# Rope rows of four tiles turned together beside the first projection, and three ada blocks on VectorE

## The chip, the core and the metric

One core of one Trainium2 chip runs the whole kernel. The metric is the device time of one execution in microseconds (us): before the change 2828.47, the median of three (2826.29 to 2839.01).

## What is computed

Two transformer blocks follow each other on 256 tokens of width 2048; the change is in the first. It needs a modulation vector, a projection, and rope on a part of its rows:

```python
mod = jax.nn.silu(c) @ w_ada[l] + b_ada[l]              # 2048 x 12288, 24 blocks of 512 columns
shift_a, scale_a, gate_a, shift_f, scale_f, gate_f = jnp.split(mod, 6, axis=-1)
h = rms_norm(x, g_attn_pre[l]) * (1.0 + scale_a[:, None]) + shift_a[:, None]
proj = h @ w_in[l]                                      # 2048 x 5456
d_q, d_k, d_v, s_q, s_k, s_v, i_q, i_k, i_w = parts     # cut from proj
rot = d // ROPE_FRACTION                                # 16 of 64 or 32 of 128 dims of a head
rotated = jnp.concatenate([x1 * cos - x2 * sin, x2 * cos + x1 * sin], axis=-1)
```

d_q, d_k, i_q and i_k have heads of 64 dims, of which rope turns 16; s_q and s_k have heads of 128, of which it turns 32. The indexer then scores keys with i_q, i_k and i_w, each query keeps 64 keys, and two kinds of attention follow.

## The kernel before

Activations lie transposed: proj is 43 tiles of 128 rows (dims) by 256 tokens, `T_DQ` 0, `T_DK` 8, `T_DV` 16, `T_SQ` 24, `T_SK` 32, `T_SV` 33, `T_IQ` 34, `T_IK` 42. All large products use float32 split in two: ScalarE rounds a weight unit into w_hi (`split`, L753), VectorE takes w_lo = raw - w_hi (`rest`, L1153), and TensorE runs three matmuls for each tile (`dense`, L1692 to L1694): x_hi w_hi, x_lo w_hi, x_hi w_lo. A unit is 4 x 128 rows by 512 columns of weights, 1 MB (1.05 million bytes).

SyncE loads the units into `raw`, a ring of four buffers (`RAW` = 4, `load`, L524): load k waits for `raw_free` of load k - 4, and all loads go through the one queue in order. w_hi and w_lo are rings of two.

The first projection walks the contraction in four parts (`K16`) and each part over 11 units of columns in the order `ORDER_IN1`; the first is a tail of 336 columns, then come the units of s_k, s_v, i_q, of s_q, of d_q, d_k and d_v. Part 0 writes proj (ScalarE, L898), parts 1 to 3 add to it (VectorE, L1311). Between them go blocks of w_ada: 512 columns are four loads (quarters), and TensorE multiplies each quarter by silu(c) right after a unit (`ada_quarter`, L1727, for units 0 to 7 of a part), ScalarE copies the sum row (`take_row`, L826), TensorE turns it into columns (`ada_columns`, L1739) and ScalarE stores them (`take_columns`, L831). So two blocks pass in each part. In the stream of loads w_in and w_ada alternate:

```python
for n, j in enumerate(ORDER_IN1):
    load(*unit("w_in", K16[part], j * COLS, in1_width(n)))
    if n < 8:
        ada(n % 4, ADA_ORDER[ADA_IN1 + 2 * part + n // 4] * COLS)
```

Parts 1 to 3 need the next quarter of x, modulated and split, which VectorE makes behind units 8 and 9 of the part before (`modulate_quarter`, `apply`).

The program of VectorE for one unit u is: `rest(u + 1)`, then the four additions of unit u, each behind its `tile_done`. The program of ScalarE is: `split(u + 1)`, then the copies that are due. TensorE runs `dense(u)`, then the ada quarter.

When all 44 units are done, rope follows for 18 steps (`turns1`): VectorE multiplies two tiles by the sines (`rotate_sin`, L1338), TensorE multiplies the product by a rotation matrix (`rotate`, L1853), GpSimd multiplies the tiles by the cosines (`rotate_cos`, L677), and VectorE adds (L1330). Rows that rope leaves alone pass through with cosine 1 and sine 0. Two ada blocks are run by TensorE between these steps. Then TensorE turns the values (`turn_values`, L1875, copied by VectorE, L1353), the indexer scores 16 heads (L1890, L1891 on TensorE; relu, L914, on ScalarE; the weighted sum, L1367, on VectorE) with two more ada blocks beside it, and the attention heads follow, with three.

After the heads, blocks of w_ada are summed by VectorE in another place (`ada_unit`, L1179 and L1181, four fused multiply-adds a quarter).

Of the kernel before, what the change touches and what calls it, by code (L numbers as in the profile page):

```python
# [36 lines left out]
COLS = 512  # L37
UK = 4
RAW = 4
# [18 lines left out]
C_ID, C_R64, C_R128, C_R64D, C_I64D, C_RM, C_COL, C_J = 0, 128, 256, 384, 512, 640, 704, 768  # L58
C_F64, C_F128, C_FM, C_ONE = 896, 897, 898, 899
# [25 lines left out]
def constants():  # L85
# [11 lines left out]
    c[:, C_R64:C_R64 + P] = rotation(64, 8, 2)  # L97
    c[:, C_R128:C_R128 + P] = rotation(128, 16, 1)
    c[:64, C_R64D:C_R64D + P] = np.tile(rotation(64, 8, 1), (1, 2))
    c[:64, C_I64D:C_I64D + P] = np.tile(np.eye(64), (1, 2))  # L100
# [13 lines left out]
    c[:, C_F64] = np.where(p % 64 < 16, freq(500000.0, 16)[p % 8], 0)  # L114
    c[:, C_F128] = np.where(p < 32, freq(500000.0, 32)[p % 16], 0)
# [24 lines left out]
ADA_ORDER = [0, 4, 1, 5, 2, 6, 3, 7, *range(8, 24)]  # L140
ADA_IN1, ADA_HEADS, ADA_OUT1, ADA_MLP1 = 2, 10, 17, 20
UNIT_HEADS = 4 * 19
UNIT_OUT1 = UNIT_HEADS + 4 * (ADA_OUT1 - ADA_HEADS)


def in1_unit(part, n):

    return 19 * part + (2 * n if n < 8 else 8 + n)
# [62 lines left out]
def program(nc, a):  # L211
    with ExitStack() as ctx:
# [12 lines left out]
        def over(start, *parts):  # L225
# [43 lines left out]
        gpad = place("gpad", [P, 4, NC])  # L269
        diag = place("diag", [P, 2, 4, P], at=gpad_at)  # L270
# [10 lines left out]
            arena, ("proj", [P, 43, S]), ("rope1", [P, 4, S]), ("posf", [P, S]), ("causal", [P, 3 * P]),  # L281
# [3 lines left out]
        vtok_at, sheets_at = arena + 4 * (43 * S + 4 * S + S + 3 * P), end - 12288  # L285
        assert vtok_at + 8 * D <= end - 12288 - 4 * 8 * S
        (rope_s, rope_c), _ = over(sheets_at, ("rope_s", [P, 2, 2, S]), ("rope_c", [P, 2, 2, S]))
# [48 lines left out]
        gain_ready = sem("gain_ready")  # L336
        lam_summed, lam_exp = sem("lam_summed"), sem("lam_exp")
# [124 lines left out]
        def pair(k):  # L462
            return rope1[:, k, :].unsqueeze(1).broadcast_to([P, 2, S])

        R64, R128 = cst[:, C_R64:C_R64 + P], cst[:, C_R128:C_R128 + P]
        RM = cst[0:64, C_RM:C_RM + 64]
        turns1 = [(proj[:, t:t + 2, :], pair(1), pair(0), R64, None, proj[:, t:t + 2, :])
                  for t in (*range(T_DQ, T_DV, 2), *range(T_IQ, T_IK, 2))]
        turns1 += [(proj[:, t:t + 2, :], pair(3), pair(2), R128, None, proj[:, t:t + 2, :])
                   for t in range(T_SQ, T_SK, 2)]  # L470
        turns1 += [(proj[:, T_SK, :], rope1[:, 3, :], rope1[:, 2, :], R128, None, proj[:, T_SK, :]),
                   (proj[0:64, T_IK, :], rope1[0:64, 1, :], rope1[0:64, 0, :], cst[0:64, C_R64D:C_R64D + P],
                    cst[0:64, C_I64D:C_I64D + P], ikk[:, :])]
# [40 lines left out]
        def _(sp):  # L514
# [92 lines left out]
        def _(pool):  # L607
# [60 lines left out]
            angles(posf[:, :], (C_F64, C_F128), P, S, rope1, sq[:, 0, 0:S], sq[:, 1, 0:S])  # L668
# [17 lines left out]
            def projected1():  # L686
                pool.wait_ge(bank_freed, BLOCKS_IN1 * 4 + 4)
                pool.wait_ge(rope_ready, 4)
            rotate_cos("one", projected1)
# [49 lines left out]
        def _(act):  # L739
# [143 lines left out]
            split(UK * in1_width(0))  # L883
            for u in range(44):
                part, n = divmod(u, 11)
                if n in (5, 9):
                    take_columns(ADA_IN1 + 2 * part + (n == 9))
# [5 lines left out]
                if n in (4, 8):  # L893
                    take_row(ADA_IN1 + 2 * part + (n == 8))
# [11 lines left out]
            for s in (ADA_HEADS, ADA_HEADS + 1):  # L906
                take_row(s)
                take_columns(s)

            for h in range(16):  # L910
# [234 lines left out]
        def _(dve):  # L1145
# [150 lines left out]

            ur.at = in1_unit(0, 0)
            rest(UK * in1_width(0))
            for u in range(44):
# [43 lines left out]
            dve.wait_ge(bank_freed, BLOCKS_IN1 * 4 + 4)  # L1343
            dve.wait_ge(rope_ready, 4)
            rotate_sin("one")

# [797 lines left out]
```

## Time and profile before

| | |
|---|---|
| median of 3 runs | 2828.47 us |
| the profiled execution, its own time | 2830.93 us |
| its span in the profile | 2829.1 us |
| TensorE busy | 2626.5 us, 93% |
| VectorE, ScalarE, GpSimd busy | 49%, 37%, 10% |
| mean granted clock of TensorE | 0.952 |
| loads of w_ada, w_in | 88 of 1 MB from the ring, 68 of 1 MB and 8 smaller ones (both projections) |

The span runs from the first instruction to the last. Times below are us from its start. PE is TensorE, PEld its weight loads, DVE VectorE, ACT ScalarE, POOL GpSimd, SPq and ACTq the instructions by which SyncE and ScalarE issue transfers. PEclk is the granted clock of TensorE as a share of 2.4 GHz. In the timeline a line gives start, length, engine, source line and operation, and in brackets the idle time before it and who ended it.

### The profile page before, as it was taken

The numbers are of one execution on the slowest core, as the hardware profiler recorded it, in microseconds if no ns is written. First come the engines' busy times: TensorE is split into PE (matmuls) and PEld (weight loads), VectorE is DVE, ScalarE is ACT, GpSimd is POOL, SyncE is SP. The second block draws the span as 40 slices with busy tenths as digits, with TensorE's granted clock in tenths as the row PEclk, the third lists the DMA queues.
The fourth block names the chain that finished last, engine by engine and source line by source line (L and its number), as shares of the span: only waits on it lengthen the run. The fifth ranks groups of instructions, "written<-read, shape, count | busy, mean of one in ns | idle before, by whom it ended". The sixth has DMA issues, their size and how long they took to land. (4 is left out here: it accounts for less than half of the span.)

```text
span 2829.1 us, 48216 instructions
## 1 busy us (share of the span) xinstructions
PE 2626.5 (93%) x20124; PEld 2402.9 (85%) x20124; DVE 1399.1 (49%) x1817; ACT 1043.2 (37%) x1327; POOL 296.6 (10%) x372
## 2 busy tenths in 40 slices
PE   5999989969999999999879979798899999999998
PEld 3888836959999999999869947358899999999998
DVE  2455565946674444344353354524455555554443
ACT  3533224334334343333233325323244444443332
POOL 4000043230000000012122000101200000000000
PEclk8999999989999999999989979778999999999999
DMA  7777765836785555555535411003455555554553
GB/s 280 263 248 274 272 238 196 316 108 215 244 289 193 179 183 188 167 191 178 174 87 178 148 38 60 30 1 117 136 175 178 182 180 181 187 178 160 182 185 111
DMA packets 260590, 501.56 MB, mean 177 GB/s; under 512 B 16160, under 2 KB 23035, under 8 KB 260219
## 3 DMA queue, kind: packets, MB, share of 16 engines
q1 hardware_dynamic: 249888, 492.99, 52.0%
q10 hardware_dynamic: 10603, 7.18, 0.9%
q8 instruction: 70, 1.15, 0.2%
q14 instruction: 29, 0.24, 0.0%
HBM read 498.05 MB, written 2.10 MB: 177 GB/s over the span
## 5 line engine op out<-in xcount | busy, mean ns | idle before, releaser
L1153 DVE TENSOR_TENSOR w_lo<-raw,w_hi 128x2048 fp32r<-128x2048 f32 (+2 forms) x386 | 862.6, 2235 | 1077.1 <-ACT w_hi L753 1077.1
L1692 PE MATMUL bank<-x_hi,w_hi 128*128 128x256 f32 (+3 forms) x4608 | 1313.8, 285 | 51.8 <-DVE w_lo L1153 17.8
L1693 PE MATMUL bank<-x_lo,w_hi 128*128 128x256 f32 (+3 forms) x4608 | 1308.7, 284 | 0.0
L1694 PE MATMUL bank<-x_hi,w_lo 128*128 128x256 f32 (+3 forms) x4608 | 1308.4, 284 | 0.0
L753 ACT ACTIVATE w_hi<-raw 128x2048 fp32r<-128x2048 f32 (+2 forms) x386 | 719.1, 1864 | 1075.5 <-PE bank L1694 945.1
L1692 PEld LDWEIGHTS bank<-x_hi,w_hi 128*128 128x128 f32 (+1 forms) x4608 | 875.5, 190 | 87.9 <-issue 37.7
L1694 PEld LDWEIGHTS bank<-x_hi,w_lo 128*128 128x128 f32 (+1 forms) x4608 | 876.5, 190 | 0.0
L1693 PEld LDWEIGHTS bank<-x_lo,w_hi 128*128 128x128 f32 (+1 forms) x4608 | 872.9, 189 | 0.0
L1692 PE MATMUL bank<-hid_hi,w_hi 128*128 128x256 f32 x1408 | 400.0, 284 | 7.9 <-POOL hid_lo L648 6.6
L1693 PE MATMUL bank<-hid_lo,w_hi 128*128 128x256 f32 x1408 | 399.1, 283 | 0.0
L1694 PE MATMUL bank<-hid_hi,w_lo 128*128 128x256 f32 x1408 | 399.0, 283 | 0.0
L1692 PEld LDWEIGHTS bank<-hid_hi,w_hi 128*128 128x128 f32 x1408 | 270.9, 192 | 9.5 <-issue 7.9
L1693 PEld LDWEIGHTS bank<-hid_lo,w_hi 128*128 128x128 f32 x1408 | 271.0, 192 | 0.0
L1694 PEld LDWEIGHTS bank<-hid_hi,w_lo 128*128 128x128 f32 x1408 | 270.9, 192 | 0.0
L648 POOL TENSOR_TENSOR hid_lo<-gpad,hid_hi 128x256 f32 x88 | 60.4, 720 | 1000.8 <-ACT hid_hi L1003 501.0
L677 POOL TENSOR_TENSOR rope_c<-proj,rope 128x512 f32<-128x512 f32 (+3 forms) x27 | 36.3, 1358 | 635.3 <-DVE proj L1311 303.1
L1181 DVE SCALAR_TENSOR_TENSOR ada_acc<-raw,csilu,ada_acc 128x512 f32<-128x512 f32 x105 | 84.2, 802 | 3.0
L1807 PE MATMUL bank<-rstd_rows,cst 16*128 16x272 f32 (+5 forms) x92 | 40.7, 621 | 31.8 <-DVE rstd_rows L1252 31.8
L1727 PE MATMUL bank<-raw,csilu 128*32 128x512 f32 x480 | 65.6, 619 | 1.3 <-ACT mod L831 1.3
L1807 PEld LDWEIGHTS bank<-rstd_rows,cst 16*128 16x128 f32 (+3 forms) x92 | 27.0, 303 | 43.2 <-DVE rstd_rows L1252 34.9
L876 ACT ACTIVATE x_hi<-tmp 128x258 fp32r<-128x258 f32 (+2 forms) x62 | 25.9, 423 | 92.2 <-DVE tmp L1282 92.2
L1311 DVE TENSOR_TENSOR proj<-proj,bank 128x256 f32<-128x256 f32 (+1 forms) x129 | 47.5, 415 | 19.0 <-PE bank L1694 19.0
(261 smaller groups left out, 1553.2 us busy)
## 6 DMA issues: line engine op xcount, KB each, us to landing
raw<-in_w_ada SPq DMA_DIRECT2D x88, 1024.0 KB, 5.2
raw<-in_w_gate SPq DMA_DIRECT2D x88, 1024.0 KB, 5.2
raw<-in_w_up SPq DMA_DIRECT2D x88, 1024.0 KB, 5.2
raw<-in_w_in SPq DMA_DIRECT2D x68, 1024.0 KB, 5.7
raw<-in_w_down SPq DMA_DIRECT2D x64, 1024.0 KB, 5.0
raw<-in_w_down SPq DMA_DIRECT2D x32, 768.0 KB, 4.4
raw<-in_w_o SPq DMA_DIRECT2D x16, 1024.0 KB, 6.0
raw<-in_w_out SPq DMA_DIRECT2D x16, 1024.0 KB, 5.1
```

The costliest lines, as they stand in the source:

```text
L648: pool.tensor_tensor(lo, gpad[:, m, 0:S], hi, ALU.subtract).then_inc(hid_low, 1)
L677: pool.tensor_tensor(rope_at(rope_buf(which, 1, src), r, src), src, cos, ALU.mult).then_inc(r_cos, 1)
L753: act.activation(w_hi[ps][:, 0:width], raw[slot][:, 0:width], ACT.Copy).then_inc(hi_ready, 1)
L876: act.activation(hi, tmp[:, (n["first"]["split"] + k) % 2, 0:n["n"]], ACT.Identity, bias=shift if shift is not None else 0.0).then_inc(n_h ...
L1153: dve.tensor_tensor(w_lo[ps][:, 0:width], raw[slot][:, 0:width], w_hi[ps][:, 0:width], ALU.subtract).then_inc(raw_free[slot], 1)
L1181: ins = dve.scalar_tensor_tensor(ada_acc[:, :], w, s, ada_acc[:, :], ALU.mult, ALU.add)
L1311: dve.tensor_tensor(t_, t_, bank[m][0:rows, 0:S], ALU.add).then_inc(bank_freed, 2 if tail and m == 2 else 1)
L1692: pe.matmul(out, wh[:, k, c], hi(k0 + k), start=a0, stop=False)
L1693: pe.matmul(out, wh[:, k, c], lo(k0 + k), start=False, stop=False)
L1694: ins = pe.matmul(out, wl_[:, k, c], hi(k0 + k), start=False, stop=z)
L1727: ins = pe.matmul(bank[7][32 * k:32 * k + 32, :], csilu[:, 4 * q + k:4 * q + k + 1].broadcast_to([P, 32]), w[:, k * COLS:(k + 1) * COLS], ...
L1807: ins = pe.matmul(spread_row(name, g, P, cols), ident[0:groups, g:g + 1].broadcast_to([groups, P]), rstd_rows[0:groups, 0:cols], start=Tru ...
```

## The change

It has two parts.

Rope. Only the rows that turn are moved. ScalarE issues small transfers inside the fourth part of the projection that gather the 16 (or 32) rows of each head into full tiles: `rows_iq`, `rows_sq`, `rows_d` hold 128 rows by two tiles of 256 tokens, `rows_x` the 16 rows of i_k and the 32 of s_k. There are five such sets (`turns1` has 5 steps in place of 18). For each, GpSimd now makes both products, TensorE one rotation, VectorE one addition (`add_rows`), and ScalarE issues transfers that scatter the rows back, for i_k into the doubled key tile `ikk`. There are 30 gathers and 33 scatters, of 16 or 32 rows each. Four sets are turned beside units 5 to 10 of the fourth part, the fifth (d_k) behind the turning of the values, and the last two scatters are issued ahead of the indexer's first relu.

Ada. Parts 0 to 2 take three blocks each in place of two; the third is summed by VectorE (`ada_beside`) behind the additions of units 1, 3, 5 and 7, a quarter each, and TensorE makes its columns behind unit 10. Part 3 keeps two. The rope stage has none left in place of two, the index stage one in place of two, the heads three as before.

```diff
-ADA_ORDER = [0, 4, 1, 5, 2, 6, 3, 7, *range(8, 24)]
-ADA_IN1, ADA_HEADS, ADA_OUT1, ADA_MLP1 = 2, 10, 17, 20
+ADA_ORDER = [0, 4, 1, 5, 8, 2, 6, 9, 3, 7, *range(10, 24)]
+ADA_IN1, ADA_LAST, ADA_INDEX, ADA_HEADS, ADA_OUT1, ADA_MLP1 = 2, 11, 13, 14, 17, 20
+def beside(part):
+    return part < 3
+def ada_of(part, which):
+    return ADA_IN1 + 3 * part + which
...
                     if n < 8:
-                        ada(n % 4, ADA_ORDER[ADA_IN1 + 2 * part + n // 4] * COLS)
-            for s in range(ADA_HEADS, ADA_OUT1):
+                        ada(n % 4, ADA_ORDER[ada_of(part, n // 4)] * COLS)
+                        if beside(part) and n % 2:
+                            ada(n // 2, ADA_ORDER[ada_of(part, 2)] * COLS)
+            for s in range(ADA_INDEX, ADA_OUT1):
...
-            rotate_cos("one", projected1)
+            for r, (src, sin, cos, _, _, _) in enumerate(turns1):
+                pool.wait_ge(rows_in[r], 16 * (2, 8, 4, 8, 8)[r])
+                if r >= 2:
+                    pool.wait_ge(r_sum, r - 1)
+                    pool.wait_ge(r_out, r - 1)
+                pool.tensor_tensor(rope_at(rope_s, r, src), src, sin, ALU.mult).then_inc(r_sin, 1)
+                pool.tensor_tensor(rope_at(rope_c, r, src), src, cos, ALU.mult).then_inc(r_cos, 1)
...
+            def gather(r, rows, tiles, dst):
+                for j in range(4):
+                    for g in range(32 // rows):
+                        act.dma_start(dst[32 * j + rows * g:32 * j + rows * g + rows, :, :],
+                                      proj[64 * g:64 * g + rows, tiles + j:tiles + 8:4, :]).then_inc(rows_in[r], 16)
...
+            def rope_rows(n):
+                done = {3: 2, 4: 3, 6: 5, 8: 7, 10: 9}
+                if n in done:
+                    act.wait_ge(bank_freed, 4 + 4 * (33 + done[n]))
...
+                elif n == 4:
+                    gather(1, 16, T_IQ, rows_iq)
+                elif n == 6:
+                    gather(2, 32, T_SQ, rows_sq)
...
+                elif n == 8:
+                    gather(3, 16, T_DQ, rows_d[:, 0:2, :])
+                elif n == 9:
+                    scatter(1, 16, T_IQ, rows_iq)
+                elif n == 10:
+                    scatter(2, 32, T_SQ, rows_sq)
+                    gather(4, 16, T_DK, rows_d[:, 2:4, :])
...
+                if n == 0 and part:
+                    take_columns(ada_of(part - 1, 2))
...
+            scatter(3, 16, T_DQ, rows_d[:, 0:2, :])
+            scatter(4, 16, T_DK, rows_d[:, 2:4, :])
...
+            def ada_beside(s, q):
+                at_ = ada_unit_at(s, q)
...
+                dve.wait_ge(raw_loaded[at_ % RAW], 16 * (at_ // RAW + 1))
+                for k in range(4):
...
+                        ins = dve.scalar_tensor_tensor(acc_beside[:, :], w, c_, acc_beside[:, :], ALU.mult, ALU.add)
...
+                ins.then_inc(raw_free[at_ % RAW], 1)
+            def add_rows(r):
+                src = turns1[r][0]
+                dve.wait_ge(r_sum, r + 1)
+                dve.wait_ge(r_cos, r + 1)
+                dve.tensor_tensor(src, turned_at(r, src), rope_at(rope_c, r, src), ALU.add).then_inc(r_out, 1)
...
+                if beside(part) and n in (1, 3, 5, 7):
+                    ada_beside(ada_of(part, 2), n // 2)
...
+                if part == 3 and n in (6, 7, 9):
+                    add_rows({6: 0, 7: 1, 9: 2}[n])
+            add_rows(3)
...
-            rotate_sin("one")
...
             take_values(0, 9, 2, lambda j: vtok[:, :, j, :])
+            add_rows(4)
...
+                if n == 10 and beside(part):
...
+                    for j in range(4):
+                        ins = pe.matmul(bank[7][:, j:j + 1], acc_beside[:, P * j:P * j + P], one(), start=True,
+                                        stop=True)
+                    ins.then_inc(ada_cols, 1)
+                if part == 3 and n in (5, 6, 8, 10):
+                    rotate_rows({5: 0, 6: 1, 8: 2, 10: 3}[n])
...
-            rotate("one")
...
+            rotate_rows(4)
+            pe.wait_ge(r_out, 4)
...
+            pe.wait_ge(rows_back[0], 16 * 5)
+            pe.wait_ge(rows_back[1], 16 * 8)
```

`rotate_rows(r)` is one matmul of the whole set by a rotation matrix. GpSimd also zeroes `rows_x` and copies the sine and cosine rows for it (four copies of 32 rows) once, early.

## Rows read from the trace of the kernel before

**Rows 1.** Stretches: length, busy times by engine, PEclk, DMA share, GB/s.
```profile
60.00:353.30 293.30, 285.79 (x2339) 254.96 (x2337) 151.15 (x205) 104.90 (x117) 0.00 (x0) 0.99 0.77 266
353.30:391.40 38.10, 34.02 (x146) 11.84 (x150) 29.78 (x46) 1.54 (x5) 28.45 (x18) 0.96 0.62 221
...
366.00:371.00 5.00, 4.40 (x16) 1.95 (x14) 4.29 (x6) 0.45 (x2) 4.60 (x4) 1.00 1.03 377
```
**Rows 2.** Waits, 60 to 353: us in total, times, longest.
```profile
ACT w_hi L753 <- DMA raw<-in_w_in: 94.3, 23, 8.0
```
**Rows 3.** Waits of the load queue, 60 to 353.
```profile
SPq L524 <- PE bank L1727: 187.3, 31, 8.5
```
**Rows 4.** Timeline of two units in part 2, from 211 to 232.
```profile
211.77 0.39 PE L1692 MATMUL bank<-x_hi,w_hi 128*128 128x256 f32 x1
...
218.65 0.39 PE L1692 MATMUL bank<-x_hi,w_hi 128*128 128x256 f32 x1
218.78 0.37 SPq L524 DMA_DIRECT2D raw<-in_w_ada  x1
219.19 0.51 SPq L524 DMA_DIRECT2D raw<-in_w_in  x1
...
226.57 1.92 ACT L753 ACTIVATE w_hi<-raw 128x2048 fp32r<-128x2048 f32 x1 [4.20 <-DMA raw<-in_w_in]
228.52 2.29 DVE L1153 TENSOR_TENSOR w_lo<-raw,w_hi 128x2048 fp32r<-128x2048 f32 x1 [2.50 <-ACT w_hi L753]
230.73 1.41 DVE L1311 TENSOR_TENSOR proj<-proj,bank 128x256 f32<-128x256 f32 x4
```
**Rows 5.** Transfers, 100 to 360: count, KB each, median us to landing.
```profile
raw<-in_w_in SPq DMA_DIRECT2D x32, 1024.0 KB, 7.4
raw<-in_w_ada SPq DMA_DIRECT2D x29, 1024.0 KB, 5.1
```
**Rows 6.** Timeline of VectorE in the output projection: one ada quarter.
```profile
513.32 3.11 DVE L1181 SCALAR_TENSOR_TENSOR ada_acc<-raw,csilu,ada_acc 128x512 f32<-128x512 f32 x4
```
**Rows 7.** Timeline of TensorE at the start of part 1.
```profile
136.57 0.36 PE L1692 MATMUL bank<-x_hi,w_hi 128*128 128x256 f32 x1 [3.74 <-DVE proj L1311]
```
**Rows 8.** The stretch behind that gap, columns as in the first group.
```profile
137.00:142.00 5.00, 5.00 (x32) 5.00 (x31) 3.04 (x4) 0.00 (x0) 0.00 (x0) 0.66 0.68 240
```
**Rows 9.** Timeline of TensorE: columns of one ada block.
```profile
340.43 0.95 PE L1739 MATMUL bank<-cst,ada_acc 128*128 128x1 f32 x8
```
**Rows 10.** Timeline from the last addition through the rope stage.
```profile
352.88 0.42 DVE L1311 TENSOR_TENSOR proj<-proj,bank 128x256 f32<-128x256 f32 x1 [0.99 <-PE bank L1694]
...
361.44 1.12 PE L1853 MATMUL bank<-rope_s,cst 128*128 128x512 f32 x2
...
362.60 0.69 DVE L1330 TENSOR_TENSOR proj<-bank,rope_c 128x512 f32<-128x512 f32 x1 [0.76 <-PE bank L1853]
...
365.43 1.65 POOL L677 TENSOR_TENSOR rope_c<-proj,rope 128x512 f32<-128x512 f32 x1 [0.41 <-DVE proj L1330]
```
**Rows 11.** Timeline of ScalarE's queue, 20 to 50: one issue.
```profile
36.39 0.44 ACTq L793 DMA_DIRECT2D packs<-in_ffn_norm_g  x1
```
**Rows 12.** The page, transfers issued by ScalarE: count, KB, us to landing.
```profile
tmp<-in_positions ACTq DMA_DIRECT2D x1, 68.0 KB, 2.8
lam_in<-in_lambda_k ACTq DMA_DIRECT2D x2, 32.0 KB, 9.5
```
**Rows 13.** Timeline of ScalarE in the index stage.
```profile
391.40 0.49 ACT L914 ACTIVATE relu<-bank 128x384 f32<-128x384 f32 x1 [7.16 <-PE bank L1891]
...
400.14 0.49 ACT L914 ACTIVATE relu<-bank 128x384 f32<-128x384 f32 x1 [0.49 <-DVE score L1367]
...
400.99 0.49 ACT L914 ACTIVATE relu<-bank 128x384 f32<-128x384 f32 x1 [0.36 <-DVE score L1367]
...
403.55 0.49 ACT L914 ACTIVATE relu<-bank 128x384 f32<-128x384 f32 x1 [1.22 <-PE bank L1891]
...
405.39 0.49 ACT L914 ACTIVATE relu<-bank 128x384 f32<-128x384 f32 x1 [1.35 <-PE bank L1891]
```

More of the change, by code:

```diff
@@ L96, in rotation @@
         return r.T
[L97 to L100, printed above, removed]
+    c[:, C_RA:C_RA + P] = rotation(16, 8, 8)
+    c[:, C_RB:C_RB + P] = rotation(32, 16, 4)
+    c[0:16, C_RX:C_RX + 16] = rotation(16, 8, 1)
+    c[32:64, C_RX + 32:C_RX + 64] = rotation(32, 16, 1)
     c[:64, C_RM:C_RM + 64] = rotation(64, 32, 1)
@@ L269, in program @@
         gpad = place("gpad", [P, 4, NC])
+        acc_beside = place("acc_beside", [P, COLS], at=gpad_at)
         diag = place("diag", [P, 2, 4, P], at=gpad_at)
@@ L284, in program @@
         assert end <= arena_end, end - arena_end
-        vtok_at, sheets_at = arena + 4 * (43 * S + 4 * S + S + 3 * P), end - 12288
+        vtok_at, sheets_at = arena + 4 * (43 * S + 6 * S + S + 3 * P), end - 12288
         assert vtok_at + 8 * D <= end - 12288 - 4 * 8 * S
+        rows_iq = place("rows_iq", [P, 2, S], at=sheets_at - 32 * S)
+        rows_sq = place("rows_sq", [P, 2, S], at=sheets_at - 24 * S)
+        rows_d = place("rows_d", [P, 4, S], at=sheets_at - 16 * S)
+        rows_x = place("rows_x", [64, S], at=vtok_at + 4 * 2 * 9 * P)
         (rope_s, rope_c), _ = over(sheets_at, ("rope_s", [P, 2, 2, S]), ("rope_c", [P, 2, 2, S]))
@@ L336, in program @@
         gain_ready = sem("gain_ready")
+        rows_in = [sem(f"rope_rows_in{r}") for r in range(5)]
+        rows_back = [sem(f"rope_rows_back{r}") for r in range(5)]
         lam_summed, lam_exp = sem("lam_summed"), sem("lam_exp")
@@ L463, in pair @@
             return rope1[:, k, :].unsqueeze(1).broadcast_to([P, 2, S])
[L465 to L473, printed above, removed]
+        RA, RB, RM = cst[:, C_RA:C_RA + P], cst[:, C_RB:C_RB + P], cst[0:64, C_RM:C_RM + 64]
+        turns1 = [(rows_x[:, :], rope1[0:64, 5, :], rope1[0:64, 4, :], cst[0:64, C_RX:C_RX + 64], None, rows_x[:, :])]
+        turns1 += [(x, pair(k + 1), pair(k), rot, None, x) for x, k, rot in (
+            (rows_iq[:, :, :], 0, RA), (rows_sq[:, :, :], 2, RB), (rows_d[:, 0:2, :], 0, RA), (rows_d[:, 2:4, :], 0, RA))]
         turns2k = [(kpg, rope2[:, 1, :], rope2[:, 0, :], RM, None, kpg)]
@@ L667, in _ @@
             chain(pool.tensor_copy(posf[:, :], pos_i[:, :]))
-            angles(posf[:, :], (C_F64, C_F128), P, S, rope1, sq[:, 0, 0:S], sq[:, 1, 0:S])
+            angles(posf[:, :], (C_FA, C_FB), P, S, rope1[:, 0:4, :], sq[:, 0, 0:S], sq[:, 1, 0:S])
+            pool.wait_ge(rope_ready, 4)
+            pool.memset(rows_x[:, :], 0.0).then_inc(cleared, 1)
+            pool.wait_ge(cleared, 4)
+            for k in range(2):
+                chain(pool.tensor_copy(rope1[0:32, 4 + k, :], rope1[0:32, k, :]))
+                chain(pool.tensor_copy(rope1[32:64, 4 + k, :], rope1[32:64, 2 + k, :]))
             def rotate_cos(which, after):
@@ L893, in _ @@
                 if n in (4, 8):
-                    take_row(ADA_IN1 + 2 * part + (n == 8))
+                    take_row(ada_of(part, int(n == 8)))
+                if part == 3:
+                    rope_rows(n)
                 if part == 0:
@@ L1821, in quarters, with rotate_rows @@
                 return ready
+            def rotate_rows(r):
+                src, _, _, rot, _, dst = turns1[r]
+                pe.wait_ge(r_sin, r + 1)
+                if r >= 2:
+                    pe.wait_ge(r_out, r - 1)
+                flat = rope_at(rope_s, r, src)
+                flat = flat.rearrange("p t n -> p (t n)") if len(flat.shape) == 3 else flat
+                pe.matmul(bank[4 + r % 2][0:dst.shape[0], 0:int(np.prod(dst.shape[1:]))], rot, flat, start=True,
+                          stop=True).then_inc(r_sum, 1)
             ada_quarter(1, 0)
@@ L1834, in _ @@
                 if n in (4, 8):
-                    ada_columns(ADA_IN1 + 2 * part + (n == 8))
+                    ada_columns(ada_of(part, int(n == 8)))
                 if n < 8:
-                    ada_quarter(ADA_IN1 + 2 * part + n // 4, n % 4)
+                    ada_quarter(ada_of(part, n // 4), n % 4)
+                if n == 10 and beside(part):
+                    s = ada_of(part, 2)
+                    last = ada_unit_at(s, 3)
+                    pe.wait_ge(raw_free[last % RAW], last // RAW + 1)
+                    pe.wait_ge(ada_copied, s)
+                    for j in range(4):
+                        ins = pe.matmul(bank[7][:, j:j + 1], acc_beside[:, P * j:P * j + P], one(), start=True,
[3 more added lines that the diff above has]
+                    rotate_rows({5: 0, 6: 1, 8: 2, 10: 3}[n])
                 if u == 10:
@@ L1859, in rotate @@
                     ins.then_inc(r_sum, 1)
-                    if which == "one" and j % 8 in (1, 2, 3, 4) and j < 16:
-                        ada_quarter(ADA_HEADS + j // 8, j % 8 - 1)
-                    elif which == "one" and j % 8 == 7:
-                        ada_columns(ADA_HEADS + j // 8)
-            rotate("one")
             def turn_values(first, tiles, meta):
@@ L1984, in _ @@
             pe.wait_ge(iw_ready, 1)
+            pe.wait_ge(rows_back[2], 16 * 4)
+            for r in (3, 4):
+                pe.wait_ge(rows_back[r], 16 * 8)
             heads(0, 16)
```

97 lines of the change are left out of this document (60 added, 37 removed).

## The prediction

> **What bounds the kernel now.** I read the busy times first: TensorE is busy 93% of the span (table above), so what counts is what makes it wait. Then the stretches that the change touches [rows 1]: the first projection (60 to 353) has TensorE busy for 285.8 of 293.3 us, and the DMA engines at 0.77. The 38.1 us behind it, rope and the turning of the values, are a hole: the loop between VectorE, GpSimd and TensorE. That hole is what the change goes after. A stretch of TensorE at 97% leaves nothing to gain, only to lose, so the next question is what almost makes it wait. The waits say it: ScalarE's w_hi stood 23 times, 94.3 us in all, for a w_in load [rows 2]; and the load queue (SyncE) stood 31 times, 187.3 us, for a TensorE ada quarter [rows 3], that is for a free raw buffer and not for bandwidth. The timeline of one unit [rows 4] gives the slack. Units start every 6.88 us (211.77, 218.65). The w_in load issued at 219.19 is taken up by ScalarE at 226.57; w_hi takes 1.92, w_lo 2.29 and ends at 230.81; the unit that needs it starts two periods after 218.65, at 232.4. So a load is on time by 1.6 us.
>
> **The ring of four raw buffers.** Load k waits until load k-4 has been read, and no load overtakes another. Call W(n), A(n), B the loads of w_in unit n, of TensorE's ada quarter n and of VectorE's. Before, W(n) at place 2n waits for W(n-2) and stands behind A(n-1), which waits for A(n-3): it goes out two units before its use. After, the order is W0 A0 W1 A1 B0 W2 A2 W3 A3 B1 W4. W2 now waits for A0, W3 for A1, W4 for A2: every W(n), n from 2 to 8, waits for A(n-2), so it goes out a whole unit later, with 1.6 us of slack.
>
> Prices. A load alone lands 5.1 us after its issue, the second of a pair 7.4 [rows 5]. In a stretch where the engines were full they moved 377 GB/s [rows 1], 2.8 us for 1.05 MB; so each load ahead in the queue costs 2.8. One ada quarter on VectorE takes 3.1 [rows 6]; I take this, and not the busy 0.8 x 4, because its row holds the chain.
>
> First late unit: A0 is read when the next unit starts (211.77 in part 2). W2 goes out at 211.9, lands 217.0, then 0.1 + 1.92 + 0.03 + 2.29 gives 221.35 against 218.65: **+2.7**, in each of three parts.
>
> Then a cycle over two units, from the end of w_lo(n), n even, in parts 1 and 2. VectorE has the four additions of the unit before, 1.41 [rows 4], queued behind the late w_lo, then B, 3.1: 4.5. Only that frees the slot for A(n+1), and the next B goes out right behind it. W(n+2) is allowed at 7.0, when A(n) has been read, but finds both ahead of it: A lands at 4.65 + 5.1 = 9.75, B at 12.55, W at 15.35. With w_hi and w_lo (4.34) the cycle is 19.7 us, where two units take 13.75: **+5.95**. In part 0 ScalarE does the additions, so 18.3 and **+4.55**. There are three cycles in a part (to n = 4, 6, 8); odd units follow on time; W9 and W10 wait for loads long read. Sum: 3 x 2.7 + 3 x 4.55 + 6 x 5.95 = **+57.5**. Part 3 has no B and runs as now. VectorE's 38 us of ada work itself costs nothing: it lies in waits for w_hi (2.50 us before 228.52 [rows 4], more where w_hi is late).
>
> Smaller terms. In parts 1 and 2 the next unit needs a bank whose addition now stands behind the late w_lo: 2 x 0.4 = **+0.8**. TensorE idles 5 us before each of these units. The one like gap of the trace, 3.74 us before 136.57 [rows 7], was followed by a stretch with the granted clock at 0.66 of full [rows 8], part of it at 1.2 GHz: (1 - 0.66) x 5 = 1.7 us lost. Inside the cycle that is hidden (TensorE has 5 us to spare and W(n+2) is held by the queue), behind the last late unit of a part it is not: 3 x 1.7 = **+5.1**. Columns of the VectorE blocks: eight small matmuls, 0.95 [rows 9], and their gap, three times: **+3.1**. ScalarE's copies for them lie in its idle time; if they did not, 0.2 each. Rotations inside part 3: one of 64 rows and half the columns 0.7 and two of 128x512 at 1.12 [rows 10] and a gap each: **+3.1**. GpSimd's ten products (1.65 each) and VectorE's additions (0.69 each) have 17 us between gather and use and cost nothing there; the last set is below. The 63 issues of ScalarE in and behind part 3 are 0.44 each [rows 11], at most eight or so (3.8 us) in a unit of 6.9 with 1.9 of w_hi: hidden, until the last unit. Their new waits (for an addition two units back, for a sum of rows) stand ahead of the next w_hi, and each is met about a unit before ScalarE comes to it; if one were late, w_hi and with it the next unit would be, us for us beyond 1.6.
>
> Behind the projection. In the coordinates of before: the last addition starts at 352.88 [rows 10], so that of unit 9 ends at 347.6, and the third set of rows is added at 348.3. ScalarE then issues 4 + 8 transfers of 0.47, until 353.95. The last gather lands after 2.8 (68 KB) by the nearest row, 9.5 by the worst (32 KB under full load) [rows 12]; the ring is full and the DMA engines idle there, so I take 2.8: 356.75. GpSimd: sine and cosine, 3.3; the addition 0.7: 360.8. ScalarE issues 8 scatters: 364.6, and the first relu comes at 364.7, where now it is 391.40: **-26.7**. The value turns and TensorE's last rotation end by 360.1, inside that. Index stage: a head beside an ada quarter takes 1.84 (403.55 to 405.39), one without 0.85 (400.14 to 400.99) [rows 13]. Four heads lose their quarter, 4 x 0.99, and TensorE does most of the other four while ScalarE still issues: **-6.8**.
>
> **Sum.** 57.5 + 0.8 + 5.1 + 3.1 + 3.1 - 26.7 - 6.8 = +36.1 on the profiled execution's 2830.9 us: 2867. The median of the runs shown lies 2.5 below that execution: 2864.
>
> What pages say beside this. The Trainium skill, page "TensorE: Matmul & The Clock Gate", section on clock-gate oscillation, holds that a loop which waits for a transfer before each burst of matmuls starts every burst at the slow clock. One row (136.57) agrees, and the gap of 2.7 us before n = 2 would tell if shorter ones do too; this is my third rival. The Trainium skill, page "DMA: Bandwidth & Descriptors", rules for kernel authors, says that transfers under 64 KB are mostly overhead. The 32 KB gathers are such; in the trace 68 KB landed in 2.8 us and 1 MB in 5.1, which agrees, and it speaks against the change.
>
> **Rivals.**
> 1. The ring does not bind: the three loads fit in, as 0.77 of the DMA engines' time seems to leave room. Then -33.5 + 3.1 + 3.1 = -27.3, 2801 us. It decides for faster once the twelve late units cost less than 1.1 us each (27.3 less the 14 of a measurable gain, over 12). Against it: the 1.6 us of slack, and that the place in the queue moves by a full 6.9. Chance 0.09.
> 2. The slot binds, the queue does not (VectorE takes B early, or loads side by side all land in 5.1): 12 late units at 2.7 = 32.4, no cold clock: 32.4 + 0.8 + 6.2 - 33.5 = +5.9, 2834. For it: the B quarter is short; against it: 7.4 for the second of a pair. Chance 0.13.
> 3. The clock falls at each gap and stays low for a whole pair: a unit takes 11.3, A(n) is read at 13.4, the cycle is 23: 9 x 3.3 = +30 and some 8 us more in units 9 and 10, about 2900. Against it: 0.66 over five us is a clock that was low for two thirds of them, not for a pair. Chance 0.10.
> 4. The rows come late (gathers at 9.5, scatters held up): +7 to +15, 2871 to 2879. Chance 0.05.
> My forecast keeps 0.63.
>
> **How the numbers follow.** 2864 is the likeliest case. Its own range, with the landing at 4.0 to 5.5 and no or double clock loss, is 2848 to 2882. The range to hold 8 in 10 reaches down to rival 2 and up to just short of rival 3: 2833 to 2894. A measurement of this kernel tells 0.5% (14 us, 2814 to 2843) from no change: faster is rival 1, 0.09; same is rival 2, 0.13; slower is the rest, 0.78.
>
> **What the profile after would show.** Right: the first quarter of the projection takes some 93 us and the next two 97 each, in place of 74, the fourth some 77; TensorE waits for w_lo before n = 2, 4, 6 and 8, 2.7 and then 5 to 6 us; loads before even units land some 8 us after their issue; the first relu comes about 27 us sooner behind the last addition. Wrong: w_in waits of ScalarE that stay at 94 us in all, or parts of 75 us. If the units wait by 2.7 only, rival 2 holds; if the clock stands near 0.5 through the parts, rival 3.

## The result, and the profile after

The changed kernel takes 2866.01 us (median of 4 runs, 2861.14 to 2872.52) where the kernel before takes 2829.14 (4 runs, 2826.29 to 2839.01): a ratio of 1.0126, interval 1.0091 to 1.016. It is 37 us slower; the forecast was 2864. Its profiled execution took 2862.18 us, with a span of 2860.4 and a mean granted clock of 0.947.

Four marks cut the span: the start of the last addition of the projection, the first relu of the index stage, the causal addition that ends that stage, and the end.

| us from the start | before | after | difference | forecast |
|---|---|---|---|---|
| last addition | 352.9 | 421.4 | +68.5 | +69.6 |
| first relu | 391.4 | 435.3 | +43.9 | +42.9 |
| causal addition | 412.9 | 449.2 | +36.3 | +36.1 |
| end of the span | 2829.1 | 2860.4 | +31.3 | +36.1 |

The stretches of after that answer to [rows 1] (length, busy time and count of PE, PEld, DVE, ACT and POOL, PEclk, DMA share, GB/s):

```profile
60.00:421.40 361.40, 310.95 (x2374) 277.24 (x2375) 187.29 (x255) 105.09 (x120) 12.97 (x13) 0.93 0.74 255
421.40:435.30 13.90, 11.62 (x68) 5.05 (x67) 5.25 (x13) 0.03 (x1) 2.48 (x2) 1.00 0.42 110
435.30:449.20 13.90, 11.42 (x73) 7.32 (x73) 11.74 (x32) 9.29 (x19) 0.00 (x0) 0.88 0.76 248
```

The hole behind the projection shrank from 38.1 to 13.9 us, but the projection has 50 us in which TensorE does nothing (361.4 less 311.0; 7.5 before), a clock of 0.93, and moves fewer bytes per us (255 GB/s, 266 before). More loads, and less bandwidth used: that speaks against the bandwidth as the limit. The waits of after up to 420 us say what it is (total, times, longest), beside [rows 2, 3]:

```profile
SPq L541 <- PE bank L1831: 191.6, 32, 9.7
SPq L541 <- DVE acc_beside L1386: 69.8, 12, 9.8
SPq L541 <- DVE w_lo L1226: 58.2, 13, 8.8
...
ACT w_hi L781 <- DMA raw<-in_w_in: 170.6, 28, 12.4
...
PE bank L1796 <- DVE proj L1412: 34.0, 11, 6.4
PE bank L1796 <- DVE w_lo L1226: 12.5, 5, 4.4
```

ScalarE waits 170.6 us for w_in where it waited 94.3. The load queue has a new wait, twelve times, for VectorE's last product of a quarter (acc_beside): the slot that forecast and code make the path. TensorE's waits for "proj" end with the first addition behind a late w_lo, about 0.5 us after it (w_lo ends at 279.56 below, TensorE goes on at 280.04); so they are waits for w_lo.

Two cycles of part 2 from the timeline of after:

```profile
257.09 2.29 DVE L1226 TENSOR_TENSOR w_lo<-raw,w_hi 128x2048 fp32r<-128x2048 f32 x1 [7.03 <-ACT w_hi L781]
259.30 1.40 DVE L1412 TENSOR_TENSOR proj<-proj,bank 128x256 f32<-128x256 f32 x4
260.62 0.48 DVE L1384 TENSOR_SCALAR acc_beside<-raw,csilu 128x512 f32<-128x512 f32 x1
261.14 2.33 DVE L1386 SCALAR_TENSOR_TENSOR acc_beside<-raw,csilu,acc_beside 128x512 f32<-128x512 f32 x3
...
263.49 0.92 SPq L541 DMA_DIRECT2D raw<-in_w_ada  x2
...
266.80 0.37 SPq L541 DMA_DIRECT2D raw<-in_w_in  x1
...
275.33 1.91 ACT L781 ACTIVATE w_hi<-raw 128x2048 fp32r<-128x2048 f32 x1 [11.39 <-DMA raw<-in_w_in]
...
277.27 2.29 DVE L1226 TENSOR_TENSOR w_lo<-raw,w_hi 128x2048 fp32r<-128x2048 f32 x1 [9.68 <-ACT w_hi L781]
...
280.04 0.55 PE L1796 MATMUL bank<-x_hi,w_hi 128*128 128x256 f32 x1 [6.38 <-DVE proj L1412]
...
283.94 0.92 SPq L541 DMA_DIRECT2D raw<-in_w_ada  x2
...
290.54 0.37 SPq L541 DMA_DIRECT2D raw<-in_w_in  x1
...
296.38 1.91 ACT L781 ACTIVATE w_hi<-raw 128x2048 fp32r<-128x2048 f32 x1 [7.02 <-PE bank L1798]
```

First cycle, counted from the end of w_lo(2) at 259.38: additions, B, and then the pair A(3), B goes out at 4.1 (forecast 4.5); W(4) is allowed at 7.4 (7.0), stands behind both, and is taken at 15.95 (15.35). That is the forecast's queue. Second cycle, from 279.56: the pair at 4.4, but W(6) only at 11.0, and it lands 5.8 us later, with nothing ahead of it. There the queue is not the path; the unit of TensorE that must read A(4) is. It ran at the low clock (slices of 4 us, columns as in the stretches above):

```profile
278.00:282.00 4.00, 1.96 (x9) 1.99 (x10) 3.96 (x7) 1.36 (x1) 0.00 (x0) 0.59 0.18 65
282.00:286.00 4.00, 4.00 (x23) 4.00 (x22) 3.93 (x4) 1.04 (x2) 0.00 (x0) 0.56 0.21 32
```

The two cycles are 20.2 and 21.1 us long: near each other, by different paths. So a hit in the sum did not yet show the mechanism.

There are nine such cycles, to n = 4, 6 and 8 in parts 0 to 2. In three of them W(n+2) was allowed 7.0 to 7.5 us behind the end of w_lo(n) and taken up 7.0 to 8.5 us later, as the forecast has it for all nine. In the other six it was allowed only 8.6 to 12.1 us behind, and in four of these it was taken up 5.0 to 5.8 us after its issue, with nothing left ahead of it. In part 1 the first unit that stood for its weights was n = 3, not 2, by 4.13 us. The forecast's own signs, loads before even units landing some 8 us after their issue and waits of 5 to 6 us before n = 4, 6, 8, held in part: five of the nine loads took 7.0 to 8.5 us, and two waits were over 5 (6.38 and 5.10). Yet the cycles are 17.9 to 18.9 us long in part 0 (forecast 18.3) and 19.3 to 21.3 in parts 1 and 2 (19.7).

The tail of after, ScalarE, VectorE and GpSimd, beside [rows 10, 13]:

```profile
419.79 5.13 ACTq L916 DMA_DIRECT2D rows_d<-proj  x8
424.96 10.27 ACTq L924 DMA_DIRECT2D proj<-rows_d  x16
435.27 0.87 ACT L987 ACTIVATE relu<-bank 128x384 f32<-128x384 f32 x2 [24.20 <-issue]
...
421.41 0.42 DVE L1412 TENSOR_TENSOR proj<-proj,bank 128x256 f32<-128x256 f32 x1 [1.00 <-PE bank L1798]
...
428.97 0.69 DVE L1396 TENSOR_TENSOR rows_d<-bank,rope_c 128x512 f32<-128x512 f32 x1 [1.85 <-POOL rope_c L717]
...
426.38 1.26 POOL L716 TENSOR_TENSOR rope_s<-rows_d,rope 128x512 f32<-128x512 f32 x1 [10.24 <-DMA rows_d<-proj]
```

The stage is no longer the loop of three engines; it is ScalarE issuing 24 transfers in 15.4 us, 0.64 each.

### The profile page after: what moved, and what is told of

It is laid out like the page before. It is cut to its first block and busy times, and to the rows that moved or that the text cites. A ratio compares the mean times of both kernels' runs of the same rounds, so it can differ in the third digit from the quotient of the medians.

```text
span 2860.4 us, 48034 instructions
## 1 busy us (share of the span) xinstructions
PE 2617.7 (92%) x20000; PEld 2414.6 (84%) x20000; DVE 1409.9 (49%) x1834; ACT 1039.8 (36%) x1324; POOL 283.0 (10%) x369
## 5 line engine op out<-in xcount | busy, mean ns | idle before, releaser
L1797 PEld LDWEIGHTS bank<-x_lo,w_hi 128*128 128x128 f32 (+1 forms) x4608 | 882.0, 191 | 0.5 <-issue 0.5
L1831 PE MATMUL bank<-raw,csilu 128*32 128x512 f32 x384 | 52.9, 623 | 2.3 <-ACT mod L859 2.3
L645 POOL TENSOR_TENSOR branch_f_ssq<-branch_f 128x256 f32 x16 | 21.9, 1366 | 227.5 <-ACT branch_f L1090 225.2
```

The costliest lines, as they stand in the source:

```text
L645: chain(pool.tensor_tensor(both[:, 1, 0:n], src, src, ALU.mult))
L1797: pe.matmul(out, wh[:, k, c], lo(k0 + k), start=False, stop=False)
L1831: ins = pe.matmul(bank[7][32 * k:32 * k + 32, :], csilu[:, 4 * q + k:4 * q + k + 1].broadcast_to([P, 32]), w[:, k * COLS:(k + 1) * COLS], ...
```

## The experiments

Each mark below is that of the one profiled execution. Three runs that have the same projection set its last addition at 361.3, 361.7 and 363.1, so a difference of 2 us there says nothing. Totals of one kernel spread over 11 to 22 us.

**Own buffer for VectorE's loads.** The ring is as before; the twelve loads go to 1 MB of their own, at the place of the rope rows, which are not needed yet. They also leave one place later than in the changed kernel; what the place alone is worth comes further below.

```diff
 load W(n)
+if beside(part) and n in (2, 4, 6, 8):
+    sp.wait_ge(beside_free, ...); sp.dma_start(raw_beside, w_ada quarter)
 if n < 8:
     ada(n % 4, ...)
-    if beside(part) and n % 2:
-        ada(n // 2, ...)
```

> The changed kernel with VectorE's twelve w_ada loads taken out of the ring of four: each goes into a 1 MB tile of its own (the place of rows_iq, rows_sq and rows_d, idle until part 3) and is issued behind W(n+1), n odd. Loads, bytes and sums are the same. Ring theory (a slot of the ring is what each even unit waits for): the 57 us of late units go, the last addition comes at 359 to 365 us instead of 421.4, TensorE's gaps for w_lo in the parts shrink under 1.5 us each, and the time is 2803 to 2812. Bandwidth theory (381 GB/s are asked for two units, 377 were the most seen): half or more of the lateness stays, last addition at 390 or later, 2835 or more. VectorE theory (its 38 us of sums hold back w_lo): nothing changes, 2866.

Measured: 2807.04 us (6 runs, 2801.81 to 2816.93), ratio 0.9915, interval 0.9891 to 0.994. The last addition starts at 361.7. The DMA engines now move 302 GB/s over the projection, with TensorE at 292 of 302 us and a clock of 0.99:

```profile
60.00:361.70 301.70, 292.22 (x2378) 259.55 (x2375) 186.99 (x255) 105.84 (x120) 12.97 (x13) 0.99 0.87 302
```

The same loads, sums, columns and rotations cost 9 us instead of 68. Bandwidth and VectorE's work are out as causes; the place of these loads in the ring of four is the cause. This kernel is faster than both.

**No loads for VectorE.** The ring as before, and VectorE sums constants that are in SBUF: three blocks of the modulation are left out of the result.

```diff
-w = raw[at_ % RAW][:, k * COLS:(k + 1) * COLS]
+w = cst[:, 0:COLS]
```

> The changed kernel without VectorE's twelve w_ada loads; VectorE runs the same 48 multiply-adds over a resident tile, so three of the 24 blocks of the modulation are not the reference's. Ring theory and bandwidth theory: the projection ends at about 359 us (353.3 of before, 3.1 for the columns, 3.1 for the rotations), total about 2803. VectorE theory: 421 us, 2866. Against the run with a buffer of its own the difference is what the twelve loads cost as loads alone: 0 to 5 us by the ring theory.

Measured: 2808.62 us (1 run), last addition 357.0. Twelve loads outside the ring cost 4.7 us there (361.7 less 357.0, one execution each) and nothing that the total shows. What is left over before, 4.1 us, is all that columns, rotations, issues and sums cost.

**No sums.** The twelve loads stay in the ring; VectorE frees the slot after one small multiplication. The three blocks are left out.

```diff
-for k in range(4): ... tensor_scalar / scalar_tensor_tensor over 128x512
+dve.tensor_scalar(acc_beside[:, P * q:P * q + P], raw[at_ % RAW][:, 0:P], c_, None, ALU.mult)
```

> The changed kernel with the twelve loads in the ring as they are, but VectorE frees each with one small multiply (128x128) in place of four multiply-adds of 128x512; three blocks of the modulation are left out. Ring theory: the cycle of two units has the 3.1 us of sums in it, so it falls from 19.7 to 16.9 us in parts 1 and 2 and from 18.3 to 16.5 in part 0; the projection ends 20 to 24 us sooner, at about 399 us, 2844 in all, and the first late unit of a part stays late by 2.7. VectorE theory: all 57 us go, 2803. Bandwidth theory: none goes, 2866.

Measured: 2866.48 us (1 run), last addition 410.3, that is 11 us sooner than after, where the ring theory wanted 20 to 24. None of the three theories is right in size. Part 2 of this run shows why:

```profile
249.37 2.29 DVE L1226 TENSOR_TENSOR w_lo<-raw,w_hi 128x2048 fp32r<-128x2048 f32 x1 [7.14 <-ACT w_hi L781]
...
252.14 0.36 PE L1789 MATMUL bank<-x_hi,w_hi 128*128 128x256 f32 x1 [3.08 <-DVE proj L1405]
...
253.21 0.92 SPq L541 DMA_DIRECT2D raw<-in_w_ada  x2
...
260.62 0.37 SPq L541 DMA_DIRECT2D raw<-in_w_in  x1
...
265.77 1.91 ACT L781 ACTIVATE w_hi<-raw 128x2048 fp32r<-128x2048 f32 x1 [9.69 <-DMA raw<-in_w_in]
```

The pair goes out 1.5 us behind w_lo, so the queue is empty when W(4) is allowed, and it lands in 5.15 us. But it is allowed 9.0 us behind w_lo, not 7.0: the unit took 8.5 us, the clock having fallen behind the 3.08 us gap. A cycle is 18.4 us, and the next two, behind like gaps, 21.4 and 20.5. So: with the sums gone, the low clock holds the cycle in their place. The next runs test that.

**TensorE kept busy, without the sums and with them.** TensorE does matmuls into an unused bank ahead of each late unit, once in the run without sums and once in the changed kernel.

```diff
+for k in range(22 if part < 3 and n in (2, 4, 6, 8) else 0):   # the changed kernel: 22, then 40
+    pe.matmul(bank[4][:, 0:S], x_hi[:, 0, 0:P], x_hi[:, 0, 0:S], start=True, stop=True)
 dense([K16[part]], ...)
```

> As the run without sums (the twelve loads stay in the ring, VectorE does one small multiplication in place of the four sums, the three blocks of the modulation are left out), and TensorE does 22 matmuls of 128x256 (2.6 us at the full clock) into an unused bank ahead of each late unit (n = 2, 4, 6, 8 of parts 0 to 2), so that it does not idle there. Clock theory: in the run without sums the ring's cycle was held long by TensorE's clock, which fell after each gap (units of 8.5 to 10 us, so A(n) was read and W(n+2) allowed 9.0 to 9.8 us behind the late w_lo in place of 7.0). With the gap filled the clock stays at 1.0, the cycle of two units is 16.4 to 17 us in place of 18.4 to 21.4, and the last addition starts at 388 to 395 in place of 410.3; total about 2845 to 2850. Rival (the waits come from the slots and the queue alone, the clock only lies beside them): the cycle stays at 18.4 to 21.4 and the last addition at 408 to 412, total about 2866, or later by what the filler delays.

> The changed kernel with TensorE's idle time ahead of the late units filled: 22 matmuls of 128x256 (2.6 us) ahead of n = 2 and 40 (4.7 us) ahead of n = 4, 6, 8 in parts 0 to 2. Forecast's mechanism (queue: W(n+2) stands behind A(n+1) and B, whatever the clock does): the cycles stay at 18.3 (part 0) and 19.7 to 20.2, the last addition starts at 415 to 421 in place of 421.4, total 2858 to 2866. Clock theory (what holds the cycle is the unit at the low clock, as in the run without sums): the cycles fall to 17 to 18, the last addition to 400 to 408, total about 2845 to 2853.

Measured, without the sums: 2841.91 us (1 run), last addition 394.1: 16 us sooner than the same kernel without the filling (and 25 us less in all, one run against one). With the sums: 2865.88 us (4 runs, 2859.26 to 2878.64), ratio to before 1.0131, interval 1.0089 to 1.0173; last addition 413.2, 8 us sooner than after, and nothing less in all. The third stretch of the two runs without sums (length, PE busy, PEclk, DMA share, GB/s), plain first, then filled:

```profile
243.00:342.00 99.00, 83.61 (x616) 0.88 0.71 242
```

```profile
243.00:342.00 99.00, 97.03 (x793) 1.00 0.81 277
```

Without the sums and with the clock at 1.0 the cycles are 16.3 to 18.0 us (one at the start of part 1, long in the kernel before too, aside). This settles the miss of the run before: behind a wait TensorE's clock falls, the slow unit reads A(n) later, W(n+2) is allowed later, and the next wait is made by the last one.

With the sums the run has a fault: the filling costs time of its own. In parts 0 and 1 six units began 1.2 to 3.7 us later than w_lo let them, some 14 us in all, because the filling was not done (without the sums some 4 us in all). An example from part 1: w_lo(4) ends at 179.69, the 40 matmuls run from 178.97, and the unit starts at 183.86.

```profile
177.40 2.29 DVE L1226 TENSOR_TENSOR w_lo<-raw,w_hi 128x2048 fp32r<-128x2048 f32 x1 [4.42 <-ACT w_hi L781]
...
178.97 5.05 PE L1948 MATMUL bank<-x_hi 128*128 128x256 f32 x40
```

So neither its total nor its last addition tells the sums from the filling. Part 2 does: there every late unit starts 0.5 us behind its w_lo, filled or not. These are w_lo(2) and w_lo(8) of part 2, three cycles apart, first with the sums, then without, both filled:

```profile
254.62 2.29 DVE L1226 TENSOR_TENSOR w_lo<-raw,w_hi 128x2048 fp32r<-128x2048 f32 x1 [6.91 <-ACT w_hi L781]
...
313.88 2.29 DVE L1226 TENSOR_TENSOR w_lo<-raw,w_hi 128x2048 fp32r<-128x2048 f32 x1 [10.39 <-ACT w_hi L781]
```

```profile
244.10 2.29 DVE L1226 TENSOR_TENSOR w_lo<-raw,w_hi 128x2048 fp32r<-128x2048 f32 x1 [6.96 <-ACT w_hi L781]
...
295.77 2.29 DVE L1226 TENSOR_TENSOR w_lo<-raw,w_hi 128x2048 fp32r<-128x2048 f32 x1 [6.51 <-ACT w_hi L781]
```

| us for three cycles of part 2, one execution each | not filled | filled | by the ring's arithmetic |
|---|---|---|---|
| with the sums | 61.6 | 59.3 | 59.1 (3 x 19.7) |
| without the sums | 60.2 | 51.7 | 50.7 (3 x 16.9) |

With TensorE kept busy the ring does what the forecast says, with the sums and without. With them W(n+2) is allowed 7.4, 8.6 and 7.4 us behind w_lo(n), stands behind the other two loads and is taken up 7.1, 7.1 and 8.9 us later. The clock theory's cycles of 17 to 18 did not come. The low clock adds to the ring's time, 2.3 us to three cycles with the sums and 8.5 without. So the two cover each other: the sums are worth 7.6 us of three cycles with the clock held, and 1.4 with it low.

**A later place in the ring.** All loads in the ring of four, each B behind the w_in load of the next unit.

```diff
-order W0 A0 W1 A1 B0 W2 A2 W3 A3 B1 W4
+order W0 A0 W1 A1 W2 B0 A2 W3 A3 W4 B1
```

> The ring of four as in the changed kernel, the twelve loads for VectorE in it, but each one place later: the order is W0 A0 W1 A1 W2 B0 A2 W3 A3 W4 B1 A4, so B goes out behind the w_in load of the unit that starts next, and VectorE takes it at the same place of its program. Ring theory: five loads a pair still leave two units of w_in only part of their lead, W3, W5, W7 now wait for A1, A3, A5 (+2.7 each at most) but no longer stand behind a B that VectorE has held up; units late by 2 to 3 us at most, parts 81 to 85 us in place of 97 to 99, last addition 379 to 386, total 2825 to 2832, level with the kernel before. Rival (bandwidth, or any five loads in a ring of four cost the same): parts of 93 us and over, last addition above 405, total above 2850. If the order costs nothing at all: last addition 359 to 365, total about 2806.

Measured: 2841.72 us (10 runs, 2836.94 to 2859.06), ratio to before 1.0039, interval 1.0015 to 1.0063. The order alone brings back 24 of the 37 us; the ring theory wanted 10 to 17 us more. The last addition of the profiled execution, one of the slowest of the ten (2856.82), is at 394.8. The queue's wait for VectorE there, 60 to 330:

```profile
SPq L542 <- DVE acc_beside L1387: 12.4, 8, 2.5
```

The wait for acc_beside falls to 12.4 us in 8 (69.8 in 12 in the changed kernel), and now TensorE waits before n = 3 and 7, by 2.6 to 4.0 us. Ahead of n = 5 it waits 1.5 to 1.7 us, but before a column product, and not for w_lo.

**The later place, with TensorE kept busy.** The same filling ahead of n = 3, 5, 7.

> The later place in the ring, plus 22 matmuls of 128x256 (2.6 us) of TensorE into an unused bank ahead of the units that are late there (n = 3, 5, 7 of parts 0 to 2; the gaps were 2.6 to 3.0 us, and the clock fell to 0.60 in the four us around the one at 252.34). Clock theory: nine units of 2 to 3 us at the low clock come back in part, cycles of 16.4 to 17 in place of 18.2 to 18.5, last addition 380 to 387 in place of 394.8, total 2828 to 2834 in place of 2841.7, level with the kernel before. Rival (VectorE's sums end with the unit and hold the slot, whatever the clock): last addition 391 to 396, total 2838 to 2842.

Measured: 2839.49 us (10 runs, 2832.58 to 2851.89), ratio to before 1.0019, interval 0.9996 to 1.0042; last addition 392.2. The clock rises from 0.94 to 1.00 in the first part and from 0.94 to 0.98 in the third, and the last addition moves by 2.6 us only, which by the number is the rival's. But ahead of n = 5 the filling did harm. It began 0.5 to 1.3 us behind the end of w_lo there and held the unit up by 2.7 to 4.2 us, 10.5 us over the three parts. In part 2 the 22 matmuls run from 268.75 and the unit starts at 272.30:

```profile
248.55 2.29 DVE L1227 TENSOR_TENSOR w_lo<-raw,w_hi 128x2048 fp32r<-128x2048 f32 x1 [4.79 <-ACT w_hi L782]
...
265.20 2.29 DVE L1227 TENSOR_TENSOR w_lo<-raw,w_hi 128x2048 fp32r<-128x2048 f32 x1 [3.14 <-ACT w_hi L782]
...
268.75 3.70 PE L1949 MATMUL bank<-x_hi 128*128 128x256 f32 x22
```

Up to that place the cycles go as the clock theory says (16.4 to 17): from the end of w_lo(3) to that of w_lo(5) 16.3, 16.6 and 16.7 us in the three parts, where the run without filling has 17.7, 18.9 and 18.3. So this run does not decide between the two. At least a part of what my ring estimate missed in this order is the clock's; how much stays open.

**The tail: the last scatters issued by SyncE.** Own buffer, and the 16 scatters of the last two sets go from ScalarE's queue to SyncE's, behind the ada loads of the index stage.

```diff
-scatter(3, 16, T_DQ, rows_d[:, 0:2, :])   # ScalarE
-scatter(4, 16, T_DK, rows_d[:, 2:4, :])
+sp.wait_ge(r_out, r + 1); sp.dma_start(...)   # r = 3, 4, behind the loads of ADA_INDEX
```

> The kernel with the buffer of its own, and the last 16 scatters (rows of d_q and d_k) issued by SyncE, which stands idle behind the first ada block of the index stage, in place of ScalarE, where they took 10.3 us ahead of the first relu. If ScalarE's issues hold the relu: the first relu comes 5 us sooner behind the last addition (8.5 to 9 us in place of 13.4), total 4 to 5 us under the run with the buffer alone, 2798 to 2807. If the fifth set of rows holds it: no change.

Measured: 2809.78 us (6 runs, 2804.58 to 2820.79), ratio to before 0.9924, interval 0.9899 to 0.9949: level with the own buffer alone. The first relu does come 9.1 us behind the last addition instead of 13.9, and the causal addition 33.3 instead of 27.8. In this execution a head beside an ada quarter took 3.44 us (from the relu at 372.18):

```profile
375.62 0.49 ACT L1001 ACTIVATE relu<-bank 128x384 f32<-128x384 f32 x1 [2.95 <-PE bank L2028]
```

**The same, with TensorE kept busy in the tail.** Twelve matmuls ahead of its last rotation.

> As the run with own buffer and SyncE's scatters, plus 12 matmuls of 128x256 (1.4 us) of TensorE into an unused bank ahead of its last rotation, where it idled. There the clock was 0.50 from 372 to 384 and a head beside an ada quarter took 3.44 us in place of 1.84. Clock theory: the heads take 1.84 again, the causal addition comes 26 to 28 us behind the last addition in place of 33.3, total 2803 to 2806 in place of 2810, level with or 2 us below the run with own buffer. Rival (the heads are long because their ada loads are issued late by SyncE): it stays at 33 us behind, total 2810.

Measured: 2810.12 us (5 runs, 2806.84 to 2817.71), ratio to before 0.9926, interval 0.9899 to 0.9953. The heads take 1.84 us (from the relu at 370.09), and the causal addition comes 26.9 us behind, where the clock theory had it; the total stays where the rival put it:

```profile
371.94 0.49 ACT L1001 ACTIVATE relu<-bank 128x384 f32<-128x384 f32 x1 [1.35 <-PE bank L2030]
```

That the filling shortened the heads is not shown. In three executions in which ScalarE issues the scatters and nothing fills the tail (no loads, no sums, the later place) the heads beside a quarter take 3.4 us too, at a clock of 0.50, and the causal addition comes 34.0, 34.1 and 35.3 us behind; in five others with ScalarE's scatters it comes 27.5 to 28.0 us behind. Slow heads come in some executions, whoever issues the scatters, and what brings them on stays open. What the medians show is that the tail has next to nothing more to give this way. The heads before ran while ScalarE was still issuing; with the relu sooner they are done in the open: the stage takes 18.0 us in the filled run and 14.0 in that of the own buffer, so of the 5.0 us that the relu gains 4.1 are given back.

## Why the prediction was right

**The ring.** The load order and the slots are as forecast, late units follow from them, and the own buffer shows that they are the loss. TensorE waited 2.6 us for its first late unit in part 0 (2.55 in the row; 2.7 forecast). The parts grew by 17.6, 19.8 and 25.3 us at w_lo of the next part's first unit; forecast, with the columns and the lost clock, 19 and twice 24. That the whole came out at 68.5 for 69.6 is in part luck, as follows.

**Its parts, by steps from run to run at the last addition.** Columns, banks, rotations: 4.1 (357.0 less 352.9), forecast 7.0. Loads beside others: 4.7, forecast nothing. Loads in the slots, with the clock held and no sums: 32.4 (394.1 less 361.7), less up to 4 that is the filling; rival 2's price is 32.4. Sums holding the slot: 19.1 (413.2 less 394.1), of which up to 10 may be filling; forecast 25.1 (57.5 less 32.4). Clock: 8.2 (421.4 less 413.2), up to 22 if the filling's own time is taken off; forecast 5.1. Each is the difference of two neighbouring runs, so they add up to 68.5 whatever the causes are: the sum proves nothing.

**The step that was wrong** is "inside the cycle that is hidden": the forecast held that W(n+2) waits for the queue whatever TensorE does, and charged the low clock three times only. In six of the nine cycles W(n+2) was allowed late, by the unit that ran slowly behind a wait (the clock was 0.50 to 0.69 over the 4 us behind waits of 2.55 to 6.38 us); in four of them the queue was empty by then. A clock of 0.93 over 361.4 us is some 25 us short of full speed, some of it while TensorE stood idle, where 0.99 over 293.3 us before is 3. The queue that the forecast charged is real, as part 2 with TensorE kept busy shows (59.3 us for 59.1). The forecast's path carries one kind of cycle, a piece of rival 3 the other; that they are within a microsecond or two of each other is luck, and so the sum did not notice. Rival 3's price (23 us a cycle) was too high, since the clock came back before the unit was over.

**Part 3.** It grew by 5.8 us, forecast 3.1 for the rotations. One thing the forecast had at nothing, ScalarE's issues: an ada quarter of TensorE stood 1.51 us for ScalarE's copy of the columns, which came at 377.63 behind eight gathers issued from 372.38 on, and the clock was 0.61 over the 4 us from 378.

```profile
377.86 1.08 PE L1831 MATMUL bank<-raw,csilu 128*32 128x512 f32 x4 [1.51 <-ACT mod L859]
```

**The hole.** The relu moved by -24.7 relative to the last addition, forecast -26.7. An issue of ScalarE costs 0.64 where [rows 11] had 0.44, and GpSimd's product takes 1.26 where [rows 10] had 1.65. These two nearly cancel up to the addition of the fifth set, which ends 8.3 us behind the start of the last addition (7.9 forecast). But by then ScalarE is still issuing the fourth set's scatters, until 430.1, so its own 24 issues in a row set the relu, and not the fifth set; the last eight take 5.1 us in place of 3.8. The last gathers were no trouble: GpSimd started 1.5 us behind the last issue. The index stage gave 7.6, forecast 6.8.

**The gathers.** The Trainium skill, page "DMA: Bandwidth & Descriptors", rules for kernel authors, has small transfers as mostly overhead. The trace agrees, and shows whose: the 32 KB transfers land in 2.0 to 5.7 us by their medians and no wait of TensorE in part 3 is put down to a landing, while the 0.64 us to issue each is what sets the first relu.

**The rest.** Between the causal addition and the end some 5 us come back (+36.3, then +31.3). No run here aimed at it, and single executions spread by more; it stays open. Rivals 1 and 4 are out: TensorE waited for late units in each of parts 0 to 2, and in part 3 for none. Of rival 2 the load that lands alone is seen in four cycles, but not its cheap units.

## What to carry to other kernels

In a ring of buffers count how many loads go by per unit of work: five loads a pair of units in a ring of four leave no load two units of lead, whatever the bandwidth says. Here a buffer of its own for the stream that a second engine reads (1 MB, borrowed from tiles that are needed later) made 37 us of loss into some 23 of gain; a place behind the load that the next unit needs brought back 24 of the 37. And where two paths through a cycle are within a microsecond of each other, taking away one cost brings in the other: the sums were worth 7.6 us of three cycles with TensorE's clock held and 1.4 with it low. Matmuls put in to hold a clock are work too: where they outlast the wait, the run no longer tells what it was made for.

## What the runs showed that was not expected

- TensorE's clock falls towards 1.2 GHz behind a wait of 2.55 us in one place of the changed kernel (0.64 over the next 4 us, at 69.4), and stays at 1.00 behind one of 2.96 in another (at 259.9): the length of the wait alone does not say. In the tail of the run with SyncE's scatters it stayed at 0.50 through the three slices of 4 us from 372 to 384, TensorE being busy all the time.
- VectorE and GpSimd slow each other. With GpSimd's products beside it in part 3, w_lo takes 3.06 us in place of 2.29, and one product of GpSimd 3.34 in place of 1.28. That product starts while w_lo runs (380.28 to 383.21) and ends 1.16 us behind it; the full w_lo of this part that no product overlaps take 2.27 to 2.29:

```profile
380.28 2.93 DVE L1226 TENSOR_TENSOR w_lo<-raw,w_hi 128x2048 fp32r<-128x2048 f32 x1 [2.35 <-ACT w_hi L781]
...
398.73 3.06 DVE L1226 TENSOR_TENSOR w_lo<-raw,w_hi 128x2048 fp32r<-128x2048 f32 x1 [4.07 <-ACT w_hi L781]
...
381.03 3.34 POOL L717 TENSOR_TENSOR rope_c<-rows_iq,rope 128x512 f32<-128x512 f32 x1
```

- A transfer between tiles of SBUF costs ScalarE 0.64 us to issue, the load from memory in [rows 11] 0.44.
